# Hybrid attention / RG-LRU / Hyena / MoE step: half of the second modulation moved into the input projection

## The reference, cut to what matters

```python
sh1, sc1, g1, sh2, sc2, g2 = modulation(c, w_mod, b_mod)      # silu(cond) @ w_mod + b_mod, w_mod 1024 x 6144
u = layer_norm(x) * (1.0 + sc1) + sh1
q, k, v, xr, gate, hy = split_projection(u, w_in)             # w_in 1024 x 2816
att = attention(q, k, v)                                      # context: dense; latent: neighbourhood + cached context
rg, h_f, h_b = rglru(xr, gate, *rg_p, h0)                     # gates: sigmoid(xb @ wa), sigmoid(xb @ wx); scans both ways
hyo = hyena(hy, *hy_p)                                        # two long convolutions through transforms
mix = concatenate([att, rg, hyo]) @ w_out
x = layer_norm(ALPHA * x + g1 * mix, ln1_g, ln1_b)
u = layer_norm(x) * (1.0 + sc2) + sh2
x = layer_norm(ALPHA * x + g2 * hier_moe(u, *moe_p), ln2_g, ln2_b)
```

## Time and profile before

| | |
|---|---|
| median of three runs | 709.79 us (706.84, 709.79, 713.08) |
| span of the profiled execution | 706.5 us |
| its own device time | not listed apart from the three above |
| TensorE (PE) busy | 658.6 us, 93% |
| PE weight loads (PEld) | 492.3 us, 70% |
| VectorE (DVE) busy | 480.9 us, 68% |
| ScalarE (ACT) busy | 309.0 us, 44% |
| GpSimd (POOL) busy | 134.9 us, 19% |
| moved by DMA | 162.63 MB, mean 230 GB/s |

### The profile page before, as it was taken

How to read it: one execution, slowest core, us unless ns; L and a number is a source line. 1 busy time by engine, 2 the same in 40 slices (tenths; PEclk the granted TensorE clock), 3 DMA queues, 4 the chain that set the end, 5 groups by cost and what they waited for, 6 DMA issues and landing times.

```text
span 706.5 us, 9443 instructions
## 1 busy us (share of the span) xinstructions
PE 658.6 (93%) x3416; PEld 492.3 (70%) x3416; DVE 480.9 (68%) x765; ACT 309.0 (44%) x505; POOL 134.9 (19%) x112
## 2 busy tenths in 40 slices
PE   7898999999999898998999999889999999999990
PEld 2236999999999555587887784466776677766440
DVE  5937687619936636568759987757676777756177
ACT  2836222334455420277731114135656565645231
POOL 0002332446522152314100000111101110000220
PEclk9999999999999999998999999899999999999995
DMA  9880732424312987289142029658999999988462
GB/s 307 347 296 9 281 90 90 128 73 155 93 59 83 308 320 298 90 251 309 56 150 89 31 99 417 261 181 324 420 423 424 420 417 425 352 319 307 141 244 119
DMA packets 38448, 162.63 MB, mean 230 GB/s; under 512 B 4225, under 2 KB 13825, under 8 KB 25603
## 3 DMA queue, kind: packets, MB, share of 16 engines
q1 hardware_dynamic: 26088, 111.72, 43.5%
q10 hardware_dynamic: 7338, 32.09, 11.5%
q0 software_dynamic: 4976, 18.22, 6.8%
HBM read 140.23 MB, written 21.01 MB: 228 GB/s over the span
## 4 chain that ended last, share of the span: by engine, by line
PE 70%; DVE 16%; DMA 5%; ACT 4%; issue 3%; ACTq 0%; POOL 0%; DVEq 0%; SPq 0%; POOLq 0%
PE bank L1656 13%; PE bank L1352 11%; PE bank L1353 11%; PE bank L1677 7%; PE bank L1547 4%; DMA arena<-in_w_mod 3%; PE bank L1190 2%; PE bank L1449 2%; DMA arena<-in_moe_w_gu 2%; PE bank L1617 2%; PE bank L1645 2%; PE bank L1519 2%; PE bank L1403 2%; PE bank L1721 2%; PE bank L1257 2%
## 5 line engine op out<-in xcount | busy, mean ns | idle before, releaser
L2175 DVE TENSOR_TENSOR gate_up_low<-arena,gate_up_high 128x1024 fp32r<-128x1024 f32 x80 | 94.3, 1221 | 49.6 <-ACT gate_up_high L1063 46.6
L1063 ACT ACTIVATE gate_up_high<-arena 128x1024 fp32r<-128x1024 f32 x80 | 80.0, 1054 | 8.5 <-DMA arena<-in_moe_w_gu 8.4
L669 POOL TENSOR_TENSOR w_low<-arena,w_high 128x1024 fp32r<-128x1024 f32 x22 | 53.6, 2438 | 151.0 <-ACT w_high L791 151.0
L1677 PE MATMUL bank<-arena 128*128 128x512 f32 x152 | 68.5, 593 | 0.8 <-ACT arena L1107 0.7
L1656 PE MATMUL bank<-gate_up_high,xt_high 128*128 128x512 f32 x152 | 61.0, 401 | 2.3 <-DVE xt_low L2261 2.3
L791 ACT ACTIVATE w_high<-arena 128x1024 fp32r<-128x1024 f32 x22 | 23.2, 1058 | 85.3 <-PE bank L1353 74.9
L1656 PE MATMUL bank<-gate_up_high,xt_low 128*128 128x512 f32 x152 | 59.4, 390 | 0.0
L1656 PE MATMUL bank<-gate_up_low,xt_high 128*128 128x512 f32 x152 | 59.3, 390 | 0.0
L1352 PE MATMUL bank<-u_high,w_high 128*128 128x320 f32 x176 | 56.0, 318 | 0.6 <-DVE u_low L1853 0.5
L1353 PE MATMUL bank<-u_high,w_low 128*128 128x320 f32 x176 | 54.4, 309 | 0.0
L1352 PE MATMUL bank<-u_low,w_high 128*128 128x320 f32 x176 | 54.4, 309 | 0.0
(11 more groups left out here) (339 smaller groups left out, 1399.5 us busy)
## 6 DMA issues: line engine op xcount, KB each, us to landing
arena<-in_moe_w_gu SPq DMA_DIRECT2D x40, 1024.0 KB, 8.3
arena<-in_w_mod SPq DMA_DIRECT2D x24, 1024.0 KB, 7.1
arena<-in_moe_w_down ACTq DMA_DIRECT2D x13, 1024.0 KB, 9.1
arena<-in_w_in SPq DMA_DIRECT2D x11, 1024.0 KB, 5.8
y_scr<-arena ACTq DMA_DIRECT2D x19, 512.0 KB, 6.1
arena<-in_moe_w_down SPq DMA_DIRECT2D x6, 1024.0 KB, 8.5
arena<-in_x SPq DMA_DIRECT2D x10, 512.0 KB, 8.2
y_scr<-arena SPq DMA_DIRECT2D x10, 512.0 KB, 6.9
```

The lines of the kernel that those rows point to most:

```text
L669: G.tensor_tensor(WL[s_][:, :, w], ring[s_][:, :, w], WH[m % 2].bitcast(F), ALU.subtract).then_inc(wl_rdy, 1)
L1063: S.activation(WGH[j][c], raw_gu[s][:, c, :, :], ACT.Copy).then_inc(wgh_rdy, 1)
L1677: last = mm(B[4 + b][:, :], hT[j][:, k, :], raw_dn[s][:, k, b * 512:(b + 1) * 512], start=(k == 0), stop=(k == 1))
L2175: tt_(WGL[s][c], raw_gu[s][:, c, :, :], WGH[j][c].bitcast(F), ALU.subtract).then_inc(wgl_rdy, 1)
```

## The change

Blocks 0 to 7 get buffers of their own, in the memory of `VC` and `KTt` in turn. SyncE issues two of them behind each of `w_in` pieces 1 to 4, and TensorE multiplies block m − 1 behind projection tile m, for m from 1 to 8. Bank 0 is thereby taken from tile 1 on, so the gates' results move to bank 7 and bank 5 (latent tokens) and the two parts of bank 6 (context tokens); a tanh waits for both gates of its pair and a pair of gates for both tanhs of the pair before. Blocks 8 to 15 stay behind the projection, with the ring as before: none in `forward(0)`, 8 to 11 in `inverse(0)`, 12 and 13 in `forward(1)`, 14 behind it, 15 in `inverse(1)`. `rel_bias(0)` goes behind block 11, `rel_bias(1)` behind block 12. VectorE's `mod2_rows(0)` goes ahead of its work for `inverse(0)`.

```diff
--- before.py
+++ after.py
@@ -444,7 +444,9 @@
 
         flat = [r.rearrange("p a b -> p (a b)") for r in ring]
         mod1_buf = [arena[:, MTAT:MTAT + 2048], arena[:, MTAT + 2048:MTAT + 4096], flat[1]]
-        mod2_buf = [flat[1], flat[2], flat[0]]
+        mod2_early = [VC.rearrange("p a b -> p (a b)")[:, 0:2048], KTt.rearrange("p a b -> p (a b)")[:, 0:2048]]
+        mod2_late = [flat[1], flat[2], flat[0]]
+        mod2_buf = [mod2_early[b % 2] if b < KT else mod2_late[(b - KT) % 3] for b in range(2 * KT)]
 
         def wait_w_in(eng, p):
 
@@ -507,18 +509,25 @@
                 eng.dma_start(flat[p % 2], t["w_in"][p * P:(p + 1) * P, :]).then_inc(win_in[p % 2], 16)
 
             def mod2_block(b):
-                if b < 3:
-                    eng.wait_ge(proj_mm, 22 if b else 20)
+                if b < 2:
+                    eng.wait_ge(spec_mm, 9)
+                elif b < KT:
+                    eng.wait_ge(mod2_mm, b - 1)
+                elif b < KT + 3:
+                    eng.wait_ge(proj_mm, 22 if b > KT else 20)
                 else:
                     eng.wait_ge(mod2_mm, b - 2)
                 k, c0 = b % KT, 2048 * (1 + b // KT)
-                eng.dma_start(mod2_buf[b % 3], t["w_mod"][k * P:(k + 1) * P, c0:c0 + 2048]).then_inc(mod_in[b % 3], 16)
+                eng.dma_start(mod2_buf[b], t["w_mod"][k * P:(k + 1) * P, c0:c0 + 2048]).then_inc(mod_in[b % 3], 16)
 
             for k in range(KT):
                 mod1_block(k)
             for p in range(11):
                 w_in_piece(p)
                 clears(p) if p < 10 else None
+                if 1 <= p < 5:
+                    for b in range(2):
+                        mod2_block(2 * p - 2 + b)
             def rel_bias(g):
                 b = g // 2
                 for h in range(4):
@@ -526,12 +535,12 @@
                                   [[8, 16], [DCPAD * 8, ROWS], [1, KW]])
                     eng.dma_start(BM[g % 3][:, h, 0:KW], src).then_inc(bm_in[g % 2], 16)
 
-            for b in range(2 * KT):
+            for b in range(KT, 2 * KT):
                 mod2_block(b)
-                if b == 4:
+                if b == KT + 3:
                     eng.wait_ge(rg_fin, 1)
                     rel_bias(0)
-                elif b == 5:
+                elif b == KT + 4:
                     rel_bias(1)
             eng.wait_ge(y_rdy, 10)
             rel_bias(2)
@@ -865,13 +874,13 @@
             def rg_tanh(c, part):
                 for m in range(4 * c + 2 * part, 4 * c + 2 * part + 2):
                     gate, e = (m % 4) // 2, m % 2
-                    eng.wait_ge(rg_mm, m + 1)
+                    eng.wait_ge(rg_mm, m // 2 * 2 + 2)
                     if m == 4 * c and c == 1:
                         eng.wait_ge(rg_out, 1)
                     hb = hbias[:, 4 * gate + 2 * e + c:4 * gate + 2 * e + c + 1]
-                    step(S.activation(RT[:, gate, e, NCTX:NTOK], B[7 if m % 2 == 0 else 0][:, :], ACT.Tanh,
+                    step(S.activation(RT[:, gate, e, NCTX:NTOK], B[5 if m % 2 else 7][:, :], ACT.Tanh,
                                       scale=0.5, bias=hb))
-                    S.activation(RT[:, gate, e, 0:NCTX], B[5 + m % 2][:, 0:NCTX], ACT.Tanh,
+                    S.activation(RT[:, gate, e, 0:NCTX], B[6][:, (m % 2) * P:(m % 2 + 1) * P], ACT.Tanh,
                                  scale=0.5, bias=hb).then_inc(rg_th, 1)
                     after(rg_th)
 
@@ -1329,11 +1338,16 @@
             def rg_gates(c, part):
                 for m in range(4 * c + 2 * part, 4 * c + 2 * part + 2):
                     gate, e = (m % 4) // 2, m % 2
-                    if m >= 2:
-                        eng.wait_ge(rg_th, m - 1)
+                    if m % 2 == 0 and m:
+                        eng.wait_ge(rg_th, m)
                     w = rgw[:, 4 * gate + 2 * e + c, :]
-                    mm(B[7 if m % 2 == 0 else 0][:, :], w, XC[:, c, 3 + NCTX:3 + NTOK], start=True, stop=True)
-                    mm(B[5 + m % 2][:, 0:NCTX], w, XC[:, c, 0:NCTX], start=True, stop=True).then_inc(rg_mm, 1)
+                    mm(B[5 if m % 2 else 7][:, :], w, XC[:, c, 3 + NCTX:3 + NTOK], start=True, stop=True)
+                    mm(B[6][:, (m % 2) * P:(m % 2 + 1) * P], w, XC[:, c, 0:NCTX], start=True, stop=True).then_inc(rg_mm, 1)
+
+            def mod2(b):
+
+                eng.wait_ge(mod_in[b % 3], 16 * ((3, 3, 2)[b % 3] + b // 3 + 1))
+                mod_block(B[b // KT], b % KT, mod2_buf[b]).then_inc(mod2_mm, 1)
 
             for m in range(22):
                 if m >= 2:
@@ -1359,6 +1373,8 @@
                     eng.wait_ge(ut_ctx, KT)
                 if 2 <= m < 8:
                     hyt(m - 2)
+                if 1 <= m <= KT:
+                    mod2(m - 1)
                 if m == 9:
                     eng.wait_ge(hyt_ev, 6)
                     eng.wait_ge(xc_rdy, 1)
@@ -1368,13 +1384,7 @@
                 if m in (16, 17):
                     rg_gates(1, m - 16)
 
-            def mod2(b):
-
-                eng.wait_ge(mod_in[b % 3], 16 * ((3, 3, 2)[b % 3] + b // 3 + 1))
-                mod_block(B[b // KT], b % KT, mod2_buf[b % 3]).then_inc(mod2_mm, 1)
-
             eng.wait_ge(rg_th, 8)
-            mod2(0)
             eng.wait_ge(proj_lat, 22)
             for i in range(TT):
                 if i == 4:
@@ -1383,7 +1393,6 @@
                     last = T.transpose(B[1 + i % 4][:, c * P:(c + 1) * P], VC[:, c, i * P:(i + 1) * P], ident)
                 last.then_inc(v_mm, 1)
 
-            mod2(1)
             eng.wait_ge(v_ev, TT)
             for c in range(4):
                 last = T.transpose(B[1][:, c * P:(c + 1) * P], KTt[:, c, 0:NCTX], ident)
@@ -1408,8 +1417,8 @@
                     last.then_inc(z_mm, 1)
                     if o == 0 and ft == 0:
                         ctx_scores()
-                    if ft in (1, 3):
-                        mod2((11 if o else 2) + ft // 2)
+                    if o and ft in (1, 3):
+                        mod2(12 + ft // 2)
 
             def ctx_scores():
 
@@ -1454,20 +1463,18 @@
                     last.then_inc(inv_mm, 1)
                     if o == 0 and i == 0:
                         ctx_values()
-                    if o == 0:
-                        for b in ((6,), (7, 8), (9, 10))[i]:
+                    if o == 0 and i < 2:
+                        for b in ((8, 9), (10, 11))[i]:
                             mod2(b)
-                    elif i < 2:
-                        mod2(14 + i)
+                    elif o and i == 0:
+                        mod2(15)
 
             eng.wait_ge(nk_ev, 1)
             forward(0)
-            mod2(4)
             ctx_turned()
-            mod2(5)
             inverse(0)
             forward(1)
-            mod2(13)
+            mod2(14)
             inverse(1)
             eng.wait_ge(z_next, 8)
             for c in range(2):
@@ -2028,7 +2035,6 @@
             for o in range(2):
                 if o:
                     token_halves()
-                    mod2_rows(0)
                 for ft in range(5):
                     eng.wait_ge(z_mm, 5 * o + ft + 1)
                     ya, yb, za, zb = ycols(ft)
@@ -2048,6 +2054,8 @@
                             V.tensor_reduce(soft[:, 0, 4 * j:4 * j + 4], B[2 - j][:, :].rearrange("p (a b) -> p a b", a=4),
                                             AX.X, ALU.max, negate=True).then_inc(s_read, 4)
                             after(s_read, 4)
+                if o == 0:
+                    mod2_rows(0)
                 for i in range(3):
                     if i < 2:
                         eng.wait_ge(half_ev, 5 + 2 * o + i + 1)
```

## The result

The kernel after takes 716.57 us in the median of 20 runs (711.75 to 722.63), the kernel before 708.46 in 20 (702.2 to 718.84). The ratio is 1.0115, with a 95% interval of 1.0091 to 1.0138: 8.1 us slower (6.4 to 9.8). The forecast was 2.4 slower, 712.2. The profiled execution of after took 720.76 us, 4.2 above its median, and its span is 717.7; the one of before has 706.5. So of the 11.2 us between the spans some 3 belong to this one execution, and I compare stage by stage, not span by span.

A forecast was written before the change was run, and what follows sets the result against it. TensorE leads the chain of waits and runs the projection without a gap; DMA share reaches 1.00 behind it. +8.6 in the projection and −6.2 behind it make +2.4 on 709.8, so 712.2 us; range 706.5 to 719.0.

The forecast's parts named there:

- Part 3: Stretch from the projection's end to hyena's end: 6.2 us shorter at full clock, 4.5 with a clock drop.
- main case: Whole kernel with TensorE at full clock behind the projection: +2.4 us, 712.2 us; chance 0.40.
- token halves at 1.43 us: VectorE's work behind the context row, before forward(1): 1.43 us, so forward(1) starts after 2.1 us idle.
- Part 1: Eight blocks put into the gapless projection cost 1.07 us each, +8.6 in all; their loads cost 0.
- Rival E: Tiling mode changes in the projection cost their upper bound: 2.7 us more, +5.1 in all, 714.9; chance 0.06.
- Rival D: Early blocks aren't early: blocks 2 to 7 stop the projection, +8 to +14 us, 718 to 724; chance 0.04.
- Part 2: The gates' new banks and waits by pairs cost 0; uncovered, up to 4 x 1.1 us.
- forward(0) to inverse(0): Behind the projection: 12.3 us for 15.75; four blocks and a DMA wait go, a wait for ACT partly replaces them.
- forward(1) to inverse(1): Blocks keep their places; if the new gap leaves TensorE at 2.4 GHz, 1.65 us come back.
- rival B: The clock drops in the new gap before forward(1): +4.1 us, 713.9; chance 0.26.
- rival A: Block 11 or the bias tables land late, queued behind block 8: up to +8.4 us, 718.2; chance 0.12.
- Rival C: Waits and clock loss behind the projection go and nothing takes their place: −5.6 us, 704.2; chance 0.11.

The follow-up runs named there:

- e2: The kernel after with early blocks 1 to 6 cut to one 32-column matmul each, all loads and waits kept; ratio 1.0024 to before, median 710.26 us.
- e3: The kernel before with only the gates' banks and their waits changed as in the change; ratio 0.9986 to before.
- e4: The kernel after with both groups of bias tables issued behind block 10, in place of behind blocks 11 and 12; ratio 1.0086 to before.
- e1: The kernel after with the eight early blocks in pairs behind projection tiles 2, 4, 6 and 8; ratio 1.0098 to before.
- e5: The kernel after with useless matmuls filling three TensorE waits: ahead of V transposes, ahead of key transposes, between inverse(0) and forward(1); ratio 1.0073 to before.
- e8: The kernel before with a fourth block buffer and the bias tables issued behind blocks 5 and 6 instead of 4 and 5; ratio 0.9922, median 702.79 us.
- e7: The kernel after with early blocks in pairs, both bias table groups behind block 10, and useless matmuls in three waits; ratio 1.0014 to before.
- e9: The kernel before with two useless matmuls between blocks 9 and 10, in the DMA wait of 2.10 us; ratio 0.9965 to before.

## Why the prediction was wrong

The direction was right, the size was not: +2.4 for +8.1. The blocks' price and the waits behind the projection came nearly as forecast; the steps that failed are the clock in Part 3, which the main case counted as a gain and which became a loss, and token halves at 1.43 us. The median of 716.57 lies within the stated range of 706.5 to 719.0, but that is no support: the range left some 3 us either way for the scatter of three runs, while the change itself is twice even the +4.1 that was forecast with a drop. Its own steps:

1. **Part 1, the price of a block, mis-sized.** 1.07 us each, 8.6 in all; measured 1.21 and 9.67, inside the stated bounds of 8.0 to 11.3. The row's own 1.07 runs from the block's start to its end; it holds neither the late start (0.09, or 0.18 behind transposes) nor what falls on the second projection matmul (0.11, or 0.02). The reading that the rows "hold two changes each" was wrong. Rival E was right that the edges cost more, with 1.1 us for its 2.7.
2. **Part 1, loads.** Cost 0: confirmed by e2. Rival D didn't happen.
3. **Part 2, the gates.** Cost 0: confirmed by e3.
4. **To forward(0), −0.3.** Measured −0.27.
5. **forward(0) to inverse(0), −3.5.** Measured −2.14. The waits for ACT and GpSimd came as forecast (e4: 12.56 us for 12.3), but this execution of after had a drop of the clock in the first tile, 1.5 us, as had those of e1 and e2. The forecast considered a drop ahead of `forward(1)` only; it counted block 0 and 1 as gone without asking what the longer waits of 1.85 and 1.53 us would do to the clock there.
6. **inverse(0) to forward(1), −0.8.** Measured −0.14. Block 11 came without a wait, as forecast. The step that failed is token halves at 1.43 us: I priced POOL's biases by when they end, not by what runs beside them. They were later than estimated as well: the second began at 282.0 where the estimate, moved by the 11.9 us by which `inverse(0)` came later, had 278.5. With the tables first (e4) the stretch takes 15.82. About 1.1 us. The cover counted for the second bias was used up too, but cost nothing: it ended at 284.36, and `inverse(1)` waited 0.22 us for GpSimd as before.
7. **forward(1) to inverse(1), −1.65 in the main case.** Measured −0.09, as in rival B. The step that failed is "if the new gap leaves it at 2.4 GHz, 1.65 us more come back", and it fails deeper than by the rival's chance: I took the drop of the earlier trace rows as a cost that before always pays, and the change could only win it back. The profile of e3 has the same gap without it. Before pays it in some executions; after, with more and longer waits, pays more: a mean clock of 0.9718 for 0.9745, **+1.5** (uncertain by 0.6) where the main case had −1.65 and rival B 0.

In sum at full clock: 9.67 in the projection, and 59.0 in the stretch (e5's 58.98) for the 63.12 that before has without a drop (e3's profile): +5.5, measured 6.2 at equal clock. The clock adds 1.5. What is left of the 8.1, 1.1, is within the intervals. Of the 5.7 us between forecast and measurement 1.1 are thus the blocks' price, 3.2 the clock and 0.4 the stretch at full clock (59.0 for 58.6). That the last is so small is partly luck: token halves took 1.0 too long, and the way to them was 0.5 shorter than I had added up (e4's 15.82 for 16.3).

Of rival A the late block didn't come; the late tables did, and cost by what their bias ran beside, not by a wait for them. Rival C, that nothing takes the waits' place, was refuted by the rows of e4: ACT and token halves stand exactly there. e2 says the same from the other side: with six of the eight blocks nearly gone from the kernel, it was at equal clock no faster than before. Its projection was still 4.74 us longer, so the stretch gave back about as much. What the eight blocks had cost where they stood can be estimated from the profiles without a drop: e8, with all sixteen blocks behind the projection, takes 60.02 us there, e5 and e4, with eight, 58.98 and 58.40. That is 1.0 to 1.6 us for eight blocks.

## What to carry to other kernels

A block of work that stands in an engine's waits is nearly free where it is (0.1 to 0.2 us here, by the estimate above); put into a stretch without idle time it costs its full price and its edges (1.21). Before loads are moved early, count what the waits for them are worth in the engine's own order of time (3.95 us here), and look for a cheaper way to the same waits: a fourth buffer took some 5 us off without touching the projection (2 to 4 at equal clock, with and without the later tables). A clock drop seen in one profile is one draw, so credit it by a share, taken from several executions' clocks.

## What the runs showed of the hardware

**VectorE waits for GpSimd.** A product of two operands in SBUF, 128x256, takes 0.41 us, and 1.43 when it starts while GpSimd's 128x1024 sum is running: it started at 276.56, GpSimd's ended at 275.36 + 2.35 = 277.71, and the product ended 0.28 later. e4, with the sum elsewhere, has all four products in 1.43. The trace of before had shown it already, in the projection (timelines of DVE and POOL; L669 makes the low half of a tile's weights, L689 is one of GpSimd's products for the RG-LRU):

```profile
179.50 4.65 DVE L1926 TENSOR_TENSOR arena<-arena 128x256 f32<-128x256 f32 x2
...
178.59 2.42 POOL L669 TENSOR_TENSOR w_low<-arena,w_high 128x1024 fp32r<-128x1024 f32 x1 [1.25 <-ACT w_high L791]
180.97 2.90 POOL L689 TENSOR_TENSOR arena<-arena 128x1280 f32<-128x1280 f32 x1
```

The first of these two products took 1.80 us and ended 0.29 after L669, the second 2.93 and ended 0.28 after L689. The Trainium skill, SBUF — State Buffer, SBUF: two separate sides, says that such an instruction and a GpSimd one lock a shared pair of ports for their whole length and the later one blocks. The trace agrees: the wait lasts until GpSimd's instruction ends. Products with one operand in PSUM aren't held up: in after the four behind `forward(1)`'s first tile (L2046 to L2049, 282.74 to 284.15) ran beside the second bias (282.00 to 284.36) in 0.41 to 0.42 us each. Such an overlap should be priced before a GpSimd step is moved.

**The clock.** With the same order of work and a gap of 2.1 us, TensorE's clock fell to 1.2 GHz in one execution and stayed at 2.4 in another. A drop cost 1.4 to 1.7 us in this stretch, and 2.8 at the start of `forward(1)` in e1 and e2. At 0.57 us per 0.001, the mean clocks of before's runs, from 0.965 to 0.982, stand for 9.7 us; their times spread by 10.2.

**What stays open.** Why e5 lost 1.3 us more than its clock explains, and which of the later stages gives e7 and e9 their higher clock, was not tried. What decides whether the fourth bias is late in the attention stays open too, and so does what a block's edges consist of.
